# Two RMS norms from one set of squares, value projections in wider items, and narrow products in four column groups, in a two-block hybrid kernel

## The chip, the cores and the metric

One core of one Trainium2 chip runs the whole program. The metric is the device time of one execution in microseconds, the median over the runs. Smaller is better.

## What is computed

The reference is a first block of two layers (a gated delta rule mixer, GDN, and a state space mixer, SSD, each followed by an expert-choice mixture of 16 experts), a final RMS norm, and a second block, which begins with an RMS norm of its own. 512 tokens and 256 context tokens of width 1024 go through it in float32. What the change touches:

```python
def rms_norm(x, g):
    xf = x.astype(F32)
    y = xf * lax.rsqrt(jnp.mean(xf * xf, axis=-1, keepdims=True) + EPS)
    return (y * g.astype(F32)).astype(x.dtype)
...
# first block, GDN mixer: the last 32 columns of the input projection
beta = jax.nn.sigmoid(p[..., off:off + 2 * GDN_HEADS].astype(F32)).reshape(b, t, 2, GDN_HEADS)
off += 2 * GDN_HEADS
g = neg_a * jax.nn.softplus(p[..., off:].astype(F32).reshape(b, t, 2, GDN_HEADS) + dt_bias.astype(F32))
...
# first block, SSD mixer
y = y.reshape(b, t, SSD_INNER).astype(h.dtype) * jax.nn.silu(z)
return rms_norm(y, norm_g) @ w_out, hf, hb
...
# end of the first block, start of the second
x = rms_norm(x, final_norm_g)
h = rms_norm_2(x, mix_norm_g[i])
(u, c_b, c_c, c_x, q, k_c, v_c, k_s, v_s, k_w, v_w, nsa_gates, mix_gates) = split_projection(h @ w_in[i])
```

## The kernel before

The tokens lie in SBUF turned: width on the 128 partitions in eight tiles (`RT[:, k, :]`, k from 0 to 7), tokens along the free axis, 256 of the context and then 512. Each engine has one program written out by hand, and semaphores tie them together. SyncE loads the weights in the order of `weight_plan` (L111) into a ring of six slots; `slots` (L162) gives each item its slot and the item whose use frees it. TensorE takes the items in the same order (`take`). A float32 product appears in the trace as two records (two passes) for one matmul.

**Norms.** `norm_sums` (PE, L1153 to 1165) sums the squares over the partitions with a matmul by ones. The tokens are cut into quarters, and each quarter goes to one group of 32 array columns and 32 PSUM partitions, so that the four products of a k stand in four column groups. ScalarE squares the even k (`norm`, L2234) and VectorE the odd (`squares`), through a ring of four buffers. Then ScalarE takes the root (L2244), VectorE the reciprocal (`reciprocal_root`, L2822), `norm_spread` (PE, L1167 to 1175) spreads it over all partitions with products of 32 rows, and VectorE scales the eight tiles (L2833, or L3484 in the second block). Call 4 is the final norm, written over `RT`; call 5 the second block's mix norm, from `RT` into `h2`; call 6 is the norm ahead of the feed-forward part. GpSimd makes ten masks (L1065 to L1079) when call 5 has scaled; TensorE waits for `nstt` and then for `mask_done` before `values`.

**Values.** `values` (PE, L1948 to 1956) makes two value projections of 128 columns and the gates' 24, for four tiles of 128 tokens: item by item, each with 32 products (8 k for each of 4 token tiles) with the normed tokens as the loaded operand. ScalarE copies each of the three out when it is done (L2633, the last with a sigmoid, L2635). `queries_keys` waits for all three.

**GDN tail.** `gdn_tail` (PE, L1190 to 1197) projects the normed tokens onto 32 columns: for each k one product of 512 moving columns and one of 256, which fill 32 of the 128 array columns. It waits for ScalarE's `h_ready` of each k (L2262). ScalarE copies the result out (L2283, L2284), TensorE turns it after the first projection tile (L1203), VectorE takes it in (L2851, L2852). The projection tiles (L1238) follow.

**SSD output.** `ssd_out` on TensorE (L1898) makes 16 gate tiles (z, in split float32, lines L1744 to L1753) and after tile i the sum of squares of tile i-2: one product by a full matrix of ones, 512 columns (L1904). ScalarE applies SiLU (L2606), squares (L2612) and scales by the norm's gain (L2613); VectorE multiplies and splits. When all 16 are summed, ScalarE takes the root over 128x512 (L2615) and VectorE the reciprocal (L3456), while TensorE is already in the output products (`sout`, 48 matmuls for each of 8 tiles of the output width, L1894). VectorE applies the reciprocal to each tile's result (L3463) and adds it to `RT` (L3466).

The experts (`experts(1)`, L1595 and others) lie between the SSD output and the final norm.

## Time and profile before

| | us |
|---|---|
| median of 3 runs | 4127.23 |
| lowest and highest run | 4116.75, 4130.4 |
| profiled execution, span from first to last instruction | 4131.5 |
| TensorE busy | 3788.0 (92%) |
| VectorE busy | 1836.7 (44%) |
| ScalarE busy | 942.2 (23%) |
| GpSimd busy | 354.9 (9%) |
| TensorE weight load busy | 2328.2 (56%) |
| mean granted TensorE clock, of full | 0.956 |

The profile gives the span of its execution and not that execution's own total time, which includes what lies around the span. Busy shares are means over stages of different kinds, and a busy TensorE need not be at its peak: pipelined matmuls overlap. In the timeline a row is one instruction or a merged run of like ones: start, duration, engine, line, operation, operands, count and, in brackets, the idle time before it with what ended it.

### The profile page before, as it was taken

How to read it: one execution, taken by the hardware profiler on the slowest of the kernel's cores; microseconds unless marked ns; L12 is line 12 of the kernel's file. 1: busy time of each engine (PE TensorE's matmuls, PEld its weight loads, DVE VectorE, ACT ScalarE, POOL GpSimd, SP SyncE). 2: the span in 40 equal slices, each digit the busy share in tenths (PEclk: the TensorE clock that was granted, in tenths of full speed). 3: DMA queues.
4: the chain of work that ended last, by engine and by line, in shares of the span. 5: the costliest groups of instructions: out<-in, count | busy, mean ns of one | idle time of the engine just before them, and what ended most of it. 6: DMA issues, size and time to landing. Idle time of an engine off the chain costs nothing.

```text
span 4131.5 us, 50603 instructions
## 1 busy us (share of the span) xinstructions
PE 3788.0 (92%) x21228; PEld 2328.2 (56%) x21228; DVE 1836.7 (44%) x2915; ACT 942.2 (23%) x1862; POOL 354.9 (9%) x929
## 2 busy tenths in 40 slices
PE   7989999998999998999988988888698998998999
PEld 4578656865534443777766762222255433446777
DVE  3656456654012221588885530111326467415443
ACT  3421133123111011456564121000115100100000
POOL 0033002301000000000000000000040157000000
PEclk8989999998999999799999989999898999999999
DMA  5241131312598896212111429999721112231331
GB/s 199 84 127 47 51 132 56 119 63 83 224 384 337 337 369 245 100 57 82 52 41 41 133 93 381 421 421 421 270 78 41 34 50 57 75 102 51 102 102 51
DMA packets 278564, 631.29 MB, mean 153 GB/s; under 512 B 63553, under 2 KB 205377, under 8 KB 219457
## 3 DMA queue, kind: packets, MB, share of 16 engines
q1 hardware_dynamic: 275712, 627.40, 41.2%
q8 instruction: 168, 2.75, 0.3%
q10 hardware_dynamic: 2624, 0.66, 0.1%
q14 instruction: 60, 0.48, 0.0%
HBM read 611.75 MB, written 16.25 MB: 152 GB/s over the span
## 4 chain that ended last, share of the span: by engine, by line
PE 67%; DMA 11%; DVE 10%; ACT 3%; POOL 3%; SPq 3%; issue 3%; ACTq 0%; DVEq 0%
PE ps L1894 11%; PE ps L1595 11%; PE ps L1238 6%; PE ps L1945 5%; PE ps L1601 4%; DMA arena<-moe_w_down 4%; DMA arena<-moe_w_gate 2%; PE ps L1502 2%; PE ps L2118 2%; PE ps L1480 2%; PE ps L1753 2%; PE ps L1748 2%; PE ps L1744 2%; DMA arena<-moe_w_up 2%; DVE arena L3488 2%
## 5 line engine op out<-in xcount | busy, mean ns | idle before, releaser
L1595 PE MATMUL ps<-arena 128*64 128x512 f32 x3072 | 709.4, 601 | 79.3 <-DMA arena<-moe_w_down 23.0
L1595 PEld LDWEIGHTS ps<-arena 128*64 128x64 f32 x3072 | 207.4, 137 | 529.4 <-issue 385.2
L3225 DVE SCALAR_TENSOR_TENSOR arena<-arena,ps 128x512 f32<-128x512 f32 (+1 forms) x48 | 30.2, 656 | 525.1 <-PE ps L1595 525.1
L1238 PE MATMUL ps<-arena 128*128 128x512 f32 (+1 forms) x768 | 253.9, 489 | 3.5 <-DVE g_rows L2882 2.1
L1945 PE MATMUL ps<-arena 128*128 128x512 f32 x512 | 229.6, 605 | 5.0 <-DVE arena L3488 4.3
L3488 DVE TENSOR_TENSOR arena<-arena,ps 128x512 f32<-128x512 f32 x86 | 58.4, 687 | 372.4 <-ACT arena L2769 143.6
L1748 PE MATMUL ps<-h_first,w_rest 128*128 128x512 f32 (+1 forms) x576 | 208.9, 379 | 0.6 <-DVE arena L3384 0.5
L1238 PEld LDWEIGHTS ps<-arena 128*128 128x128 f32 x768 | 145.9, 191 | 105.8 <-issue 93.6
L3233 DVE TENSOR_TENSOR m_yx_rest<-ps,m_yx_lead 64x512 fp32r<-64x512 f32 x64 | 44.1, 689 | 363.0 <-ACT m_yc_lead L2484 205.6
L1744 PE MATMUL ps<-h_second,w_rest 128*128 128x512 f32 (+1 forms) x576 | 196.1, 355 | 0.4 <-DVE h_second L3291 0.4
L2484 ACT ACTIVATE m_yx_lead<-ps 64x512 fp32r<-64x512 f32 x64 | 37.8, 591 | 662.3 <-PE ps L1595 661.5
L1601 PE MATMUL ps<-arena 128*32 128x256 f32 x3072 | 175.7, 380 | 0.0
L1945 PEld LDWEIGHTS ps<-arena 128*128 128x128 f32 x512 | 98.9, 195 | 134.4 <-issue 127.1
L1894 PE MATMUL ps<-h_lead,w_lead 128*128 128x512 f32 x352 | 139.7, 397 | 11.4 <-DVE h_rest L3426 6.8
L1601 PEld LDWEIGHTS ps<-arena 128*32 128x32 f32 x3072 | 94.7, 109 | 96.8 <-issue 38.9
L1894 PE MATMUL ps<-h_rest,w_lead 128*128 128x512 f32 x352 | 139.5, 396 | 0.0
L1894 PE MATMUL ps<-h_lead,w_rest 128*128 128x512 f32 x352 | 139.1, 395 | 0.0
L1045 POOL IOTA arena<- 128x64 f32 x2 | 0.4, 185 | 1523.0 <-DVE arena L3466 1388.3
L3488 DVE TENSOR_TENSOR arena<-arena 128x512 f32<-128x512 f32 (+4 forms) x181 | 126.4, 738 | 6.2 <-ACT arena L2720 2.6
L1753 PE MATMUL ps<-h_first,w_rest 128*128 128x512 f32 (+1 forms) x576 | 124.6, 359 | 0.1
L1748 PEld LDWEIGHTS ps<-h_first,w_rest 128*128 128x128 f32 x576 | 110.0, 191 | 19.8 <-issue 3.5
L1744 PEld LDWEIGHTS ps<-h_second,w_rest 128*128 128x128 f32 x576 | 108.7, 189 | 18.9 <-issue 3.1
(496 smaller groups left out, 6990.6 us busy)
## 6 DMA issues: line engine op xcount, KB each, us to landing
arena<-moe_w_gate SPq DMA_DIRECT2D x128, 1024.0 KB, 9.3
arena<-moe_w_up SPq DMA_DIRECT2D x128, 1024.0 KB, 10.7
arena<-moe_w_down SPq DMA_DIRECT2D x128, 1024.0 KB, 11.8
arena<-ada_w SPq DMA_DIRECT2D x48, 1024.0 KB, 5.0
arena<-ffn_w_gate_up SPq DMA_DIRECT2D x22, 1024.0 KB, 5.0
arena<-gdn_w_in SPq DMA_DIRECT2D x16, 1024.0 KB, 8.9
arena<-w_in SPq DMA_DIRECT2D x30, 512.0 KB, 3.8
arena<-ssd_w_x SPq DMA_DIRECT2D x8, 1024.0 KB, 4.8
```

The costliest lines, as they stand in the source:

```text
L1238: mm = pe.matmul(ps[:, 2 * (i % 2) + j, 0:nn], state.w[:, k, m * P:(m + 1) * P], hT[:, k, c0:c0 + nn], start=(k == 0), stop=(k == KD - 1))
L1480: mm = pe.matmul(ps[:, 2 + b + 2 * (j % 2), 0:nn], state.w[:, k, (j % 2) * P:(j % 2) * P + P], hT[:, k, c0:c0 + nn], start=(k == 0), stop= ...
L1502: mm = pe.matmul(ps[:, b + 2 * (m % 2), 0:nn], w[j // 2][:, j % 2, m * P:(m + 1) * P], oT[:, j, c0:c0 + nn], start=(j == 0), stop=(j == HG ...
L1595: mm = pe.matmul(ps[CAPX * h:CAPX * h + CAPX, bank, :], x[:, 0:CAPX], w[:, 512 * h:512 * h + 512], **flags)
L1601: mm = pe.matmul(ps[CAPC * q:CAPC * q + CAPC, bank, 0:CW], x[:, CAPX:SLOTS], w[:, CW * q:CW * q + CW], **flags)
L1744: rests = lambda k: pe.matmul(out, wh[:, k, cols_], hT_lo[k][:, x], start=False, stop=(tail_last and k == KD - 1))
L1748: pe.matmul(out, wh[:, k, cols_], hT_hi[k][:, x], start=(k == 0), stop=False)
L1753: mm = pe.matmul(out, wl[:, k, cols_], hT_hi[k][:, x], start=False, stop=(not tail_last and k == KD - 1))
L1894: mm = pe.matmul(out, a[:, k, cols_], tile_of(b, k), start=(k == 0 and n == 0), stop=(k == tiles - 1 and n == 2))
L1945: mm = pe.matmul(ps[:, bank, :], w[:, k, i * P:(i + 1) * P], h2[:, k, :], start=(k == 0), stop=(k == KD - 1))
L2118: mm = pe.matmul(ps[:, (3 * i + x) % 5, :], w[:, k, (i % 2) * P:(i % 2 + 1) * P], h2[:, k, :], start=(k == 0), stop=(k == KD - 1))
L3488: v.do(dve.tensor_tensor(out, a_, b_, op), sem)
```

## The change

1. The final norm and the mix norm share one set of squares. TensorE sums the squares x² as before and beside it the squares weighed with the final gain squared (`weighed`, from `gain2`). From the first root VectorE and ScalarE work out the second one: the mean square of the final-normed tokens is the weighed sum times the first factor squared. Both factors are spread together; VectorE first scales into `h2` with the product of both gains, then `RT`. Calls are renumbered (6 becomes 5).
2. The second block's values come from two items of 4 k and 280 columns (128, 128 and 24 together), so that a product moves 280 columns, and all three results are copied out after the last of 32 products.
3. The SSD output norm sums the four quarters of the tokens in four column groups; root and reciprocal work on 128 columns, and after the first output product TensorE spreads the reciprocal by four products of 32 rows; ScalarE copies it from PSUM.
4. The GDN tail's products go token tile by token tile to four column groups.

```diff
-    plan += [("bv", n) for n in range(3)]
+    plan += [("bv", n) for n in range(2)]
...
+        tail_at = lambda t: (slice(32 * (t % 4), 32 * (t % 4) + 32), slice(t // 4 * P, t // 4 * P + P))
...
-            pool.wait_ge(s.nstt, nstt0[5] + KD)
+            pool.wait_ge(s.nstt, nstt0[4] + KD)
...
             def norm_sums(call, sets, weighed=None):
...
+                    for g in range(4 if weighed is not None else 0):
+                        r = slice(32 * g, 32 * g + 32)
+                        mm = pe.matmul(ps[r, 0, P:2 * P], weighed[:, k, :], nsqb[k % 4][:, CTX + g * P:CTX + g * P + P],
+                                       start=False, stop=(k == KD - 1))
...
             def norm_spread(call, sets):
-                for c0, w, at in quarters_of(sets):
+                for w, at in [(w, at) for _, w, at in quarters_of(sets)] + ([(P, P)] if call == 4 else []):
...
             def gdn_tail():
-                    for bank, (c0, nn, _) in ((2, XSET), (3, CSET)):
-                        mm = pe.matmul(ps[0:4 * GH, bank, 0:nn], w[:, k, :], hT[:, k, c0:c0 + nn], start=(k == 0), stop=(k == KD - 1))
+                    for t in range(NT):
+                        r, c = tail_at(t)
+                        mm = pe.matmul(ps[r, 2 + t // 4, 0:P], w[:, k, :], hT[:, k, t * P:(t + 1) * P], start=(k == 0), stop=(k == KD - 1))
...
             def ssd_out():
                 def sums(i):
-                    mm = pe.matmul(ps[:, 7, :], ones, z_sq[i % 2], start=(i == 0), stop=(i == 15))
+                    for g in range(4):
+                        r = slice(32 * g, 32 * g + 32)
+                        mm = pe.matmul(ps[r, 7, 0:P], ones[:, r], z_sq[i % 2][:, g * P:(g + 1) * P], start=(i == 0), stop=(i == 15))
+                def spread():
+                    pe.wait_ge(s.root_part, 1)
+                    for g in range(4):
+                        r = slice(32 * g, 32 * g + 32)
+                        mm = pe.matmul(ps[:, 4 + g, 0:P], ones[r, :], z_rs[r, :], start=True, stop=True)
+                    mm.then_inc(s.root_part, 1)
...
                     product(ps[:, m % 2, :], w, slice(0, P), (y_hi, y_lo), SI // P, split_ready).then_inc(s.w_used, 1)
+                    if m == 0:
+                        spread()
...
             def values():
-                for n in range(3):
-                    w = take(("bv", n))
-                    nn = (P, P, 3 * NH)[n]
-                    for t in range(4):
-                        for k in range(KD):
-                            mm = pe.matmul(ps[:, n, t * nn:(t + 1) * nn], h2[:, k, t * P:(t + 1) * P], w[:, k, :],
-                                           start=(k == 0), stop=(k == KD - 1))
-                    mm.then_inc(s.w_used, 1)
+                w = [take(("bv", n)) for n in range(2)]
+                for t in range(4):
+                    for k in range(KD):
+                        mm = pe.matmul(ps[:, t, 0:VALUES], h2[:, k, t * P:(t + 1) * P], w[k // 4][:, k % 4, :],
+                                       start=(k == 0), stop=(k == KD - 1))
+                mm.then_inc(s.w_used, 2)
             def queries_keys():
                 pe.wait_ge(s.bv_out, 3)
+                pe.wait_ge(s.nstt, nstt0[4] + 2 * KD)
...
-            norm_sums(4, (XSET,))
+            norm_sums(4, (XSET,), gain2)
             norm_spread(4, (XSET,))
-            norm_sums(5, (XSET,))
-            norm_spread(5, (XSET,))
...
# ScalarE
-            a.do(act.activation(tail[:, CTX:N], ps[0:4 * GH, 2, :], ACT.Copy))
-            a.do(act.activation(tail[:, 0:CTX], ps[0:4 * GH, 3, 0:CTX], ACT.Copy), s.tl_in)
+            a.do(act.activation(tail[:, 0:P], ps[:, 2, 0:P], ACT.Copy))
+            a.do(act.activation(tail[0:64, P:2 * P], ps[0:64, 3, 0:P], ACT.Copy), s.tl_in)
...
-                a.do(act.activation(z_rt, ps[:, 7, :], ACT.Sqrt, bias=epsc, scale=1.0 / SI), s.go_rt)
+                a.do(act.activation(z_rt, ps[:, 7, 0:P], ACT.Sqrt, bias=eps32, scale=1024.0 / SI), s.go_rt)
+                act.wait_ge(s.root_part, 2)
+                a.do(act.activation(z_all.rearrange("p (g c) -> p g c", g=4), ps[:, 4:8, 0:P], ACT.Copy), s.root_part)
...
+                act.wait_ge(s.w_used, USED[("bv", 1)])
+                for n in range(2):
+                    a.do(act.activation(vS[:, n, :, :], ps[:, 0:4, n * P:(n + 1) * P], ACT.Copy), s.bv_out)
+                a.do(act.activation(ng, ps[:, 0:4, 2 * P:VALUES], ACT.Sigmoid), s.bv_out)
...
             norm(4, (XSET,))
+            act.wait_ge(s.root_part, 4)
+            a.do(act.activation(nrtb[:, 2 * P:3 * P], nrtb[:, P:2 * P], ACT.Sqrt, bias=eps32, scale=1024.0 * 1024.0 / D), s.root_part)
             act.wait_ge(s.nstt, nstt0[4] + KD)
-            norm(5, (XSET,))
...
# VectorE, SSD output
-                v.do(dve.reciprocal(z_rs, z_rt))
-                v.settle()
+                v.do(dve.reciprocal(z_rs, z_rt), s.root_part)
...
-                    v.do(dve.tensor_tensor(z_tmp[m % 2], ps[:, m % 2, :], z_rs, ALU.mult))
+                    if m == 0:
+                        dve.wait_ge(s.root_part, 3)
+                    v.do(dve.tensor_tensor(z_tmp[m % 2], ps[:, m % 2, :], z_all, ALU.mult))
...
# VectorE, after route(1), before experts(1)
+            v.do(dve.tensor_tensor(gain2, col("final", 0, KD).unsqueeze(2).to_broadcast([P, KD, 32]), col("final", 0, KD).unsqueeze(2).to_broadcast([P, KD, 32]), ALU.mult))
+            v.do(dve.tensor_tensor(col("mixn", 0, KD), col("mixn", 0, KD), col("final", 0, KD), ALU.mult))
...
+            def two_norms():
+                squares(4, (XSET,))
+                dve.wait_ge(s.nrt, 3 * 4 + 1)
+                first, t, root2 = nrsb[:, P:2 * P], nrtb[:, P:2 * P], nrtb[:, 2 * P:3 * P]
+                v.do(dve.reciprocal(first, nrtb[:, 0:P]))
+                v.settle()
+                tt(t, ps[:, 0, P:2 * P], first, ALU.mult)
+                v.settle()
+                tt(t, t, first, ALU.mult, s.root_part)
+                dve.wait_ge(s.root_part, 5)
+                v.do(dve.reciprocal(nrsb[:, 2 * P:3 * P], root2))
+                v.settle()
+                v.do(dve.scalar_tensor_tensor(out=nrsb[:, 0:P], in0=nrsb[:, 2 * P:3 * P], scalar=32.0, in1=first, op0=ALU.mult, op1=ALU.mult), s.nrt)
+                dve.wait_ge(s.nrt, 3 * 4 + 3)
+                scaled_norm("mixn", 0, lambda k: h2[:, k, :])
+                v.settle()
+                scaled_norm("final", P, lambda k: RT[:, k, CTX:N])
```

VectorE's intake of the turned tail becomes four instructions (for the first four token tiles and the last two) in place of two.

## Rows read from the trace of the kernel before

**Rows 1.** The page's chain that ended last, by engine.

```profile
PE 67%; DMA 11%; DVE 10%; ACT 3%; POOL 3%; SPq 3%; issue 3%; ACTq 0%; DVEq 0%
```

**Rows 2.** Timeline, 24 to 92 us: start us, us, engine, line, what.

```profile
41.55 13.25 PE L1196 MATMUL ps<-arena 128*32 128x512 f32 x32
...
41.86 4.15 ACT L2262 ACTIVATE arena<-arena 128x512 f32<-128x512 f32 x8 [1.92 <-DVE arena L2797]
...
54.73 10.59 PE L1238 MATMUL ps<-arena 128*128 128x512 f32 x32
```

**Rows 3.** Windows: us, busy time of each engine, PEclk (granted clock), DMA share, GB/s.

```profile
46.00:48.00 2.00, 2.00 (x7) 0.59 (x5) 0.00 (x0) 0.01 (x1) 0.00 (x0) 0.72 0.98 371
```

**Rows 4.** Timeline of TensorE, SSD gate loop.

```profile
2213.10 2.02 PE L1753 MATMUL ps<-h_first,w_rest 128*128 128x512 f32 x8
...
2218.60 2.02 PE L1753 MATMUL ps<-h_first,w_rest 128*128 128x512 f32 x8
...
2224.96 2.02 PE L1753 MATMUL ps<-h_first,w_rest 128*128 128x512 f32 x8
```

**Rows 5.** Timeline, first product of the SSD output.

```profile
2309.32 0.50 PE L1894 MATMUL ps<-y_lead,so_lead 128*128 128x512 f32 x1 [2.48 <-DVE w_rest L3426]
```

**Rows 6.** Timeline, the two norms and the start of the values.

```profile
2969.25 2.48 PE L1164 MATMUL ps<-arena 128*32 128x128 f32 x64 [1.60 <-ACT arena L2241]
...
2972.20 0.37 ACT L2244 ACTIVATE arena<-ps,arena 128x128 f32<-128x128 f32 x1
2972.60 0.95 DVE L2822 RECIPROCAL arena<-arena 128x128 f32<-128x128 f32 x1 [1.35 <-ACT arena L2244]
...
2973.60 0.50 PE L1174 MATMUL ps<-arena 32*128 32x128 f32 x8 [1.88 <-DVE arena L2822]
...
2980.25 3.64 PE L1164 MATMUL ps<-arena 128*32 128x128 f32 x64 [6.14 <-ACT arena L2241]
...
2985.37 0.81 PE L1174 MATMUL ps<-arena 32*128 32x128 f32 x8 [1.48 <-DVE arena L2822]
2986.25 5.36 DVE L3484 SCALAR_TENSOR_TENSOR arena<-arena,ps 128x512 f32<-128x512 f32 x8 [0.94 <-PE ps L1174]
...
2993.74 25.60 PE L1954 MATMUL ps<-arena 128*128 128x128 f32 x192 [7.56 <-issue]
```

**Rows 7.** Timeline, the end of the values and the first query product.

```profile
3011.12 0.60 ACT L2633 ACTIVATE arena<-ps 128x512 f32<-128x512 f32 x1 [6.55 <-PE ps L1954]
...
3011.74 1.28 ACT L2635 ACT_TABLE_LOAD   x1
...
3019.37 0.25 ACT L2635 ACTIVATE arena<-ps 128x96 f32<-128x96 f32 x1 [6.35 <-PE ps L1954]
...
3019.68 1.22 PE L1973 MATMUL ps<-arena 128*128 128x512 f32 x1 [0.34 <-ACT arena L2635]
```

**Rows 8.** Timeline of TensorE, a block in four column groups between other products.

```profile
103.62 1.46 PE L1238 MATMUL ps<-arena 128*128 128x256 f32 x6
105.01 1.93 PE L1141 MATMUL ps<-arena 128*32 128x256 f32 x32
106.88 1.12 PE L1247 MATMUL ps<-arena 128*128 128x512 f32 x2
```

**Rows 9.** Lines by form: an operation of 128 columns of VectorE on PSUM.

```profile
L3011 DVE SCALAR_TENSOR_TENSOR arena<-ps,arena 128x128 f32<-128x128 f32 x96 | 27.1, 344 | 6.9 <-PE ps L1382 6.9
```

**Rows 10.** Timeline of VectorE, first operation after the experts' start.

```profile
2501.38 0.75 DVE L3225 SCALAR_TENSOR_TENSOR arena<-arena,ps 128x512 f32<-128x512 f32 x1 [38.38 <-PE ps L1595]
```

**Rows 11.** Windows, start and end of the values: columns as rows 3.

```profile
2995.00:3000.00 5.00, 5.00 (x27) 5.00 (x27) 3.92 (x28) 1.52 (x3) 0.94 (x7) 0.54 0.00 0
3018.00:3020.00 2.00, 1.66 (x8) 1.54 (x8) 0.00 (x0) 0.25 (x1) 1.92 (x2) 0.50 0.00 0
```

**Rows 12.** Windows, then waits of SyncE's queue, in the second experts' stage.

```profile
2600.00:2700.00 100.00, 85.56 (x366) 28.32 (x366) 14.73 (x21) 7.13 (x12) 0.00 (x0) 1.00 1.01 421
...
SPq L888 <- ACT arena L2458: 56.0, 1, 56.0
```

More of the change, by code:

```diff
@@ L52 @@
 NST = 16
+VALUES = 2 * 128 + 3 * NH
 TURN = 6.2831850
@@ L315, in __init__ @@
         self.s_st = new("s_st")
+        self.root_part = new("root_part")
         self.sz_act = new("sz_act")
@@ L709, in source2 @@
             if kind == "bv":
-                a, w = ((WVS, P), (WVW, P), (WNG, 24))[item[1]]
-                return whole(win[:, :, a:a + w])
+                k = slice(4 * item[1], 4 * item[1] + 4)
+                return [((lambda w: w[:, :, 0:P]), win[:, k, WVS:WVS + P]), ((lambda w: w[:, :, P:VALUES]), win[:, k, WVW:WVW + P + 3 * NH])]
             if kind == "bq":
@@ L751, in shape_of @@
                 return (4, HD)
+            if item[0] == "bv":
+                return (4, VALUES)
             if item[0] == "glu":
@@ L1151, in ada_turn, with norm_sums @@
                 mm.then_inc(s.ada_cols, 1)
-            def norm_sums(call, sets):
+            def norm_sums(call, sets, weighed=None):
                 parts = quarters_of(sets)
@@ L1164, in norm_sums @@
                             mm = pe.matmul(ps[r, 0, at:at + w], ones[:, r], nsqb[k % 4][:, c0 + g * w:c0 + g * w + w],
-                                           start=(k == 0 and at == 0), stop=(k == KD - 1 and at == parts[-1][2]))
+                                           start=(k == 0 and at == 0), stop=(k == KD - 1 and at == parts[-1][2] and weighed is None))
+                    for g in range(4 if weighed is not None else 0):
+                        r = slice(32 * g, 32 * g + 32)
+                        mm = pe.matmul(ps[r, 0, P:2 * P], weighed[:, k, :], nsqb[k % 4][:, CTX + g * P:CTX + g * P + P],
+                                       start=False, stop=(k == KD - 1))
                     mm.then_inc(s.nsq_sum, 1)
@@ L1202, in gdn_tail_turned @@
                 for t in range(NT):
-                    mm = pe.transpose(ps[:, 6, 32 * t:32 * t + 32], tail[:, t * P:(t + 1) * P], ident[0:4 * GH, 0:4 * GH])
+                    r, c = tail_at(t)
+                    mm = pe.transpose(ps[:, 4 + t % 4, 32 * (t // 4):32 * (t // 4) + 32], tail[r, c], ident[r, r])
                 mm.then_inc(s.tl_in, 1)
@@ L2784, in _ @@
             act.wait_ge(s.resid, RES_SSD + KD)
-            norm(6, (XSET,))
+            norm(5, (XSET,))
             ffn()
@@ L2850, in _ @@
             dve.wait_ge(s.tl_in, 2)
[L2851 to L2853 removed]
+            for t0, nt in ((0, 4), (4, 2)):
+                turned = ps[:, 4:4 + nt, 8 * t0:8 * t0 + 32]
+                v.do(dve.tensor_copy(betag[:, t0:t0 + nt, 0:16], turned[:, :, 0:16]))
+                v.do(dve.tensor_tensor(betag[:, t0:t0 + nt, 16:32], turned[:, :, 16:32],
+                                       col("gdtb", 0, 16).unsqueeze(1).to_broadcast([P, nt, 16]), ALU.add), s.tl_bias if t0 else None)
             dve.wait_ge(s.tl_act, 1)
@@ L3475, in _, with scaled_norm @@
             route(1)
+            v.do(dve.tensor_tensor(gain2, col("final", 0, KD).unsqueeze(2).to_broadcast([P, KD, 32]), col("final", 0, KD).unsqueeze(2).to_broadcast([P, KD, 32]), ALU.mult))
+            v.do(dve.tensor_tensor(col("mixn", 0, KD), col("mixn", 0, KD), col("final", 0, KD), ALU.mult))
+            v.settle()
             experts(1)
-            def norm2(call, gain, dst):
-                if call != 6:
-                    squares(call, (XSET,))
-                reciprocal_root(call, (XSET,))
+            def scaled_norm(gain, at, dst):
                 for k in range(KD):
-                    v.do(dve.scalar_tensor_tensor(out=fours(dst(k)), in0=fours(RT[:, k, CTX:N]), scalar=col(gain, k), in1=spread_root(SEQ // 4, 0),
+                    v.do(dve.scalar_tensor_tensor(out=fours(dst(k)), in0=fours(RT[:, k, CTX:N]), scalar=col(gain, k), in1=spread_root(SEQ // 4, at),
                                                   op0=ALU.mult, op1=ALU.mult), s.nstt)
+            def two_norms():
[13 more added lines that the diff above has]
+                scaled_norm("mixn", 0, lambda k: h2[:, k, :])
+                v.settle()
+                scaled_norm("final", P, lambda k: RT[:, k, CTX:N])
             def tt(out, a_, b_, op, sem=None):
@@ L3792, in ffn @@
                         split(f[:, i % 8, :], tile_of(f_hi, i), tile_of(f_lo, i), s.ff_hid)
-            norm2(4, "final", lambda k: RT[:, k, CTX:N])
-            norm2(5, "mixn", lambda k: h2[:, k, :])
+            two_norms()
             dve.wait_ge(s.mask_done, MASKS + 10)
@@ L3803, in _ @@
             mix()
-            squares(6, (XSET,))
+            squares(5, (XSET,))
             split_unit(0)
-            norm2(6, "ffnn", lambda k: h2[:, k, :])
+            reciprocal_root(5, (XSET,))
+            scaled_norm("ffnn", 0, lambda k: h2[:, k, :])
             ffn()
```

23 lines of the change are left out of this document (7 added, 16 removed).

## The prediction

> **What bounds the kernel now.** I read the page's chain by engine first [rows 1]: TensorE carries 67% of it, DMA 11%, VectorE 10%. So a change on TensorE counts in full unless a stage between is set by DMA. The change touches four places, and I read each in the timeline, in order of time. The granted clock I took from the windows, because TensorE's durations double when it falls: 1.00 is 2.4 GHz, 0.50 is 1.2 GHz.
>
> The GDN tail [rows 2] is a block of 32 records from 41.55 us, and the first projection tile follows it at 54.73. That tile moves just as many columns (16 records of 512 and 16 of 256, 12288 in all) and lasts 10.59 us, or 0.86 ns for a column of a record. I use this rate at full clock throughout. The tail took 13.2 us because the clock was low until about 47.1 (a mean of 0.72 over 46 to 48, [rows 3]).
>
> In the SSD gate loop a tile without a sum takes 5.50 us (2213.10 to 2218.60) and one with a sum 6.36 (to 2224.96) [rows 4]: a sum costs 0.86. There TensorE never stops. After the loop it waits 2.48 us for VectorE's splitting of the first output weight [rows 5].
>
> Between the blocks everything is a relay. The first norm's sums start at 2969.25, the second norm's last scaling ends at 2991.61, and the wait for GpSimd's masks, which the code puts behind it, holds TensorE until 2993.74 [rows 6]. Then 192 records of values take until 3019.36 and the queries start at 3019.68 [rows 6, 7].
>
> **GDN tail.** The same products go to four groups of 32 array columns, six tiles of 128 tokens per k. That four groups run side by side is in the trace: 32 records of 256 columns take from 105.01 to 106.88 [rows 8], 1.87 us, where 8192 columns in line would take 7.0. Six tiles need two rounds, so a k costs 2 x 2 x 128 x 0.86 = 0.44 us at full clock, 0.88 at the low one. Starting at 41.55 with the clock low to 47.1, 6.3 of the 8 k's are done by then and the other 1.7 take 0.75: end 47.9, and I give the projection 48.0. ScalarE's h tiles end at 46.01 [rows 2], so they allow this. Gain 54.73 - 48.0 = 6.7. Bounds: 7.7 if only h limits it (46.01 plus one k), and 4.3 if the clock stays low another 3.4 us, which costs 0.7 in the tail and 1.7 in the tile behind. The tail's copies on ScalarE shrink and two instructions more on VectorE (under 0.3 us each) sit in its long wait; its next step is held by TensorE's second tile, so all that shifts as one. The later weights need the tail's slot earlier, and get it.
>
> **SSD norm.** A sum becomes four products of 128 columns, 8 records: 8 x 128 / 4 x 0.86 = 0.22 us. Row evidence on going into the narrow shape and out: six records of 256 columns from 103.62 should end at 104.94 and the grouped block begins at 105.01, 0.07 late; the block itself holds 1.75 us of work and takes 1.87, 0.12 more [rows 8]. So 0.42 per sum, 0.44 less. Sums 0 to 12 stand ahead of the last gate product, so 13 x 0.44 = 5.7. The last three hide behind VectorE's split, which keeps its 2.48 us wait. New on the path is the spreading behind the first output product: 8 records, 0.50 [rows 6], and 0.2 for changing shape, 0.7. The reciprocal shrinks to a quarter of its columns and ScalarE's copy of 512 columns (0.60, [rows 7]) comes in; VectorE waits for it, but TensorE needs its result only before the third output product, and the whole second one lies between, so both cost nothing. If that cover went, they would cost 0.6. Net 5.0. Bounds: 7.8 with no price for changing shape, and a loss of 0.7 if each sum costs what it did.
>
> The page "TensorEngine Tiling (Array Packing)" of the Trainium skill, section Tiling Modes, says that changing the tiling mode drains TensorE. The rows just read show 0.2 us for both changes together, which is compatible with a drain and small; were a full drain to eat the saving of every sum, the sum over all parts would be that of the first rival below.
>
> **Final norm and mix norm.** Removed: a second round of squares, sums, root and spreading, and the second block of eight scalings (5.36) from the path, since the final scaling now runs behind the mix one, beside the values. Added on the path, by steps from 2969.25: 128 records of sums instead of 64, at full clock 8 x 0.44 = 3.5 and 0.25 to finish, 2973.0 (the old ones, 2.48 us, were paced by the squares; the root stood ready at 2972.20 behind its table load, so 0.8 later). Root 0.37, reciprocal 0.95, two multiplies of 128 columns at 0.34 (nearest row, a VectorE operation of that size on PSUM [rows 9]), second root 0.37, second reciprocal 0.95, one more 0.34, and 0.05 at each of seven handovers: 4.0, so 2977.0. Spreading two sets at the clock that by then is low: 0.81 for one [rows 6], 1.25 for two. Eight scalings 5.36: 2983.7. Gain 2991.6 - 2983.7 = 7.9. Bounds: 8.7 with the spreading at full clock and cheap multiplies, 3.3 if the sums run at the low clock (3.64 for 64 records [rows 6], 7.3 for 128) and the multiplies cost double. GpSimd's masks still start after the mix norm, so their 2.1 us stay, now beside VectorE's final scaling: 0 to 2 us more; I take 0. The two gain products before the experts fall in a gap of VectorE of 38 us [rows 10]; cost 0. VectorE's preparation for the S5 part starts behind the final scaling, about as early as before, and its user, the S5 part, comes only behind the attention.
>
> **Values.** 64 records of 280 columns: 64 x 280 x 0.86 = 15.4 us. The clock was low from before 2993.74 to about 2999.7 (0.54 in [rows 11]); a wait of the same kind precedes it, so I keep 6 us at half speed, 3.0: 18.4. But all three copies come after the last product, where two were hidden: 2 x 0.60, the table load 1.28, the sigmoid 0.25 and handovers, 2.8 us in which TensorE stands, for 0.3 before [rows 7]. The old block of 24 columns ended at low clock (0.50 [rows 11]) and the queries began so; the new stall probably leaves them a similar start, so they cost the same. 25.94 - 18.4 - 2.8 = 4.7. Bounds 7.7 (full clock from the start) and 1.7 (low clock for 6 us more).
>
> The page "ScalarE: Activation LUTs" of the Trainium skill, section What ACT_TABLE_LOAD costs, adds about 1.38 us of drain to a load of 1.28. The row of the load and its neighbours show 1.28 with the next operation free at once; with the page's drain this part would give 3.3 and not 4.7.
>
> **Sum.** 6.7 + 5.0 + 7.9 + 4.7 = 24.3 us. The profiled execution has a span of 4131.5; its own total is not shown, and the span is 4.3 over the median of the runs, 4127.2. From the span I get 4107.2, from the median 4102.9. I forecast 4103.
>
> **The rivals.**
> 1. *Changing shape eats the sums.* SSD then gives -0.7 and not 5.0: 4108.5. For it: 26 changes in a loop with no slack. Against: the 0.2 us read from [rows 8]. Chance 0.12.
> 2. *The clock stays low longer* behind the tail, in the norm and behind the values' stall: by the lower bounds of three parts 4.3 + 5.0 + 3.3 + 1.7 = 14.3: 4113. Chance 0.12.
> 3. *The experts' DMA absorbs what comes before it.* In that stage the queues run at 421 GB/s, share 1.01, and TensorE waits for them [rows 12]. If the stream's start were fixed, the 11.7 us of tail and SSD would vanish: 4114.5, no measurable change or just faster. Against: SyncE waits 56 us for ScalarE's last copy of the routing before the stream can run [rows 12], and that copy moves with TensorE. Chance 0.06.
> 4. *Slower: the gate loop falls to the low clock.* Its place is the sixteen gate tiles, 94 us of TensorE at 5.9 each, at the pace of the full clock now. If the shape changes in each tile brought the clock down, each microsecond at 1.2 GHz would cost half of one; from 49 us of low clock on the change loses, and with the whole loop low it takes 94 us more: 4197. Against: the grouped block of [rows 8] ran at the pace of the full clock, and so did what followed it. Chance 0.04.
> 5. *The groups do not overlap where PSUM banks are shared by six tiles:* tail 0, SSD -3.9, norm near 0, values 4.7: 4126. The block of [rows 8] is nearly proof against it; 0.02.
>
> **How the numbers follow.** The forecast has 0.64 (4095 to 4108). A measurement here tells about 0.3%, 12.4 us, from no change: faster means under 4114.8. Forecast and rivals 1 and 2, with most of 3, are on that side, the upper ends of 2 and 3 and rival 5 within it. The range takes in all upper bounds (7.7 + 7.8 + 8.7 + 7.7 = 31.9: 4095) with 5 us under them for the spread of the runs (4116.75 to 4130.4), so 4090; up to 4117 it holds rivals 1, 2 and 3, and leaves out little more than both low cases at once (4.3 - 0.7 + 3.3 + 1.7 = 8.6: 4119) and rivals 4 and 5.
>
> **What would show it.** Tail 6 to 7 us long with the first tile at about 48; gate tiles every 5.9 us; from the first sum to the last mix scaling 14.5 us (22.4 before), with two roots and one spreading in it; values 18 us, then a gap of 2.8 with the table load in it. Gate tiles still at 6.3 speak for rival 1, a clock of 0.50 in their windows for 4, a saving at the first expert product that is gone at the last for 3. The forecast is wrong if the spans of these four stages do not shrink by 20 us together.

## The result, and the profile after

The changed kernel takes 4108.85 us (median of 11 runs, 4096.63 to 4120.73), the kernel before 4130.95 on the same chip (11 runs, 4116.75 to 4139.22). The ratio is 0.9945, 95% interval [0.9932, 0.9958]: 22.1 us less, where 24.3 had been worked out. One execution further below, of the changed kernel run again, was in a slower state of the chip (4170.65 us, granted clock 0.912) and counts in no number. The profiled execution took 4111.48 us and has a span of 4109.5, 22.0 less than the span before. Its mean granted clock is the same, 0.956.

The page after (busy times of the engines, and the chain by engine). TensorE is busy 21.0 us less (3788.0 before) in a span that is 22.0 shorter; its share of the chain is what it was [rows 1]:

```profile
span 4109.5 us, 50683 instructions
PE 3767.0 (92%) x21268; PEld 2313.8 (56%) x21268; DVE 1833.0 (45%) x2918; ACT 940.0 (23%) x1859; POOL 354.8 (9%) x929
...
PE 67%; DMA 11%; DVE 10%; POOL 3%; ACT 3%; SPq 3%; issue 3%; ACTq 0%; DVEq 0%
```

**GDN tail.** Timeline after, to set against [rows 2] (start, duration, engine, line, operands, count):

```profile
43.09 6.26 PE L1207 MATMUL ps<-arena 128*32 128x128 f32 x96
...
49.28 10.59 PE L1250 MATMUL ps<-arena 128*128 128x512 f32 x32
```

From the first tail product to the first projection tile it is 6.19 us, before 13.18 (41.55 to 54.73). The stage gave 7.0. It started 1.5 us later than before, although nothing ahead of it had changed. That comes with the execution: the kernel with the norms alone, whose tail is the old one, starts it at 43.17, and the changed kernel with its sums in pairs at 41.96. In windows of the same trace the clock is 0.50 over 40 to 47 us and 0.65 over 47 to 49: nearly the whole tail still ran at 1.2 GHz, and four groups side by side made it short all the same.

**SSD gate loop and its sums.** Timeline of TensorE after, to set against [rows 4] and [rows 5]:

```profile
2217.20 2.02 PE L1765 MATMUL ps<-h_first,w_rest 128*128 128x512 f32 x8
...
2283.95 2.02 PE L1765 MATMUL ps<-h_first,w_rest 128*128 128x512 f32 x8
2285.91 0.43 PE L1918 MATMUL ps<-arena 128*32 128x128 f32 x8
2286.26 0.50 PE L1760 MATMUL ps<-h_first,w_rest 128*128 128x512 f32 x1
2286.60 0.39 PE L1756 MATMUL ps<-h_second,w_rest 128*128 128x512 f32 x1
...
2296.09 2.02 PE L1765 MATMUL ps<-h_first,w_rest 128*128 128x512 f32 x8
...
2304.05 0.79 PE L1906 MATMUL ps<-y_lead,so_lead 128*128 128x512 f32 x1 [3.18 <-DVE w_rest L3449]
```

L1765 at 2217.20 is the end of the last tile without a sum, 2296.09 that of the sixteenth: 78.89 us for 13 tiles, 6.07 each. A tile without a sum takes 5.50 here too, so a sum costs 0.57 (0.86 before). It can be seen where: the eight products of a tile's last group take 1.86 us, so they are done with at 2285.81; the group starts 0.10 later, the next gate product starts at 2286.26, 0.45 later, and the one behind it 0.34 after that instead of 0.23. From the same mark of the loop to the first output product it is 90.72 us before (2218.60 to 2309.32) and 86.85 now: 3.9 less. The first output product still waits for VectorE's split, now 3.18 us instead of 2.48. It comes 7.96 us after the mark of the sixteenth tile in both kernels (2301.36 to 2309.32 before, 2296.09 to 2304.05): what stands behind the last gate tile is covered by that wait.

**The norms.** Timeline after, to set against [rows 6]; the sums of the two norms alternate (L1170 the plain ones, L1174 the weighed ones, 0.43 us for a block of eight):

```profile
2963.79 0.43 PE L1170 MATMUL ps<-arena 128*32 128x128 f32 x8 [1.60 <-ACT arena L2262]
2964.01 0.43 PE L1174 MATMUL ps<-arena 128*32 128x128 f32 x8
...
2967.55 0.37 ACT L2265 ACTIVATE arena<-ps,arena 128x128 f32<-128x128 f32 x1 [0.25 <-PE ps L1174]
2967.95 0.95 DVE L3517 RECIPROCAL arena<-arena 128x128 f32<-128x128 f32 x1 [1.45 <-ACT arena L2265]
...
2969.59 0.40 ACT L2795 ACTIVATE arena<-arena 128x128 f32<-128x128 f32 x1 [1.67 <-DVE arena L3532]
...
2971.01 0.29 DVE L3525 SCALAR_TENSOR_TENSOR arena<-arena 128x128 f32<-128x128 f32 x1
2971.36 1.24 PE L1184 MATMUL ps<-arena 32*128 32x128 f32 x16 [3.86 <-DVE arena L3525]
2972.66 10.75 DVE L3508 SCALAR_TENSOR_TENSOR arena<-arena,ps 128x512 f32<-128x512 f32 x16 [1.36 <-PE ps L1184]
...
2978.08 0.16 POOL L1071 MEMSET arena<- 128x64 f32 x1 [553.26 <-DVE arena L3508]
...
2980.16 5.14 PE L1976 MATMUL ps<-arena 128*128 128x280 f32 x13 [7.56 <-DVE arena L3508]
```

Half of the sixteen scalings end at 2972.66 + 10.75/2 = 2978.03, and GpSimd starts its masks 0.05 later. From the first sum to there it is 14.2 us, before 22.4 (2969.25 to 2991.61). The wait for the masks is still behind it, 2.1 us.

**Values.** The values and the query products in the timeline of TensorE (192 records in 25.60 us before, then 0.3 us of idling, [rows 6, 7]):

```profile
2980.16 17.17 PE L1976 MATMUL ps<-arena 128*128 128x280 f32 x64 [7.56 <-DVE arena L3508]
3000.06 29.43 PE L1996 MATMUL ps<-arena 128*128 128x512 f32 x64 [2.74 <-ACT arena L2656]
```

ScalarE's rows between them:

```profile
2997.36 1.08 ACT L2655 ACTIVATE arena<-ps 128x512 f32<-128x512 f32 x2 [9.52 <-PE ps L1976]
2998.46 1.28 ACT L2656 ACT_TABLE_LOAD   x1
2999.76 0.25 ACT L2656 ACTIVATE arena<-ps 128x96 f32<-128x96 f32 x1
```

The windows of every engine behind them (columns: length, busy time and count of TensorE, its weight loads, VectorE, ScalarE, GpSimd; granted clock; DMA share; GB/s):

```profile
3000.00:3002.00 2.00, 1.94 (x4) 0.88 (x5) 0.00 (x0) 0.01 (x1) 1.76 (x5) 0.73 1.15 320
3002.00:3004.00 2.00, 2.00 (x4) 0.96 (x3) 0.00 (x0) 0.00 (x0) 1.84 (x4) 0.50 0.17 40
```

64 records take 17.2 us, then TensorE stands 2.7 us, and the queries start at 3000.06, 19.9 us after the values (25.94 before). The clock is 1.00 up to 3000 and falls inside the next window: some of the first query products ran at 1.2 GHz, as the first ones did before, where the clock had fallen already in the products of 24 columns (0.68 over 3016 to 3018, ahead of the idling). The 64 query records take 29.4 us, and 29.6 before.

**The sum.** Tail 7.0, norms 8.1, values 6.0, and SSD 3.2 (3.9 in the loop less the spreading, below) make 24.3 us; the span is 22.0 shorter. The rest is in stages that the change does not touch. From the first projection tile to the first router product it is 928.0 us before and 931.3 after. This is no matter of the clock, which is low for about 3 us less there; TensorE is idle 4.6 us longer, and its waits that end with the transfer into `low_in` (a small matrix of the GDN layer that goes out to memory and back) come to 8.3 us and not 3.2. The changed kernel is ahead by 5.5 us at the first projection tile, 2.1 at the router, 1.4 at the mark of the gate loop, 5.3 at the first output product, 5.5 at the end of the experts, 13.6 at the values, 19.6 at the queries and 22.0 at the end.

### The profile page after: what moved, and what is told of

It is laid out like the page before. It is cut to its first block, busy times and chain, and to the rows that moved or that the text cites. A ratio compares the mean times of both kernels' runs of the same rounds, so it can differ in the third digit from the quotient of the medians.

```text
span 4109.5 us, 50683 instructions
## 1 busy us (share of the span) xinstructions
PE 3767.0 (92%) x21268; PEld 2313.8 (56%) x21268; DVE 1833.0 (45%) x2918; ACT 940.0 (23%) x1859; POOL 354.8 (9%) x929
## 4 chain that ended last, share of the span: by engine, by line
PE 67%; DMA 11%; DVE 10%; POOL 3%; ACT 3%; SPq 3%; issue 3%; ACTq 0%; DVEq 0%
PE ps L1607 11%; PE ps L1906 11%; PE ps L1250 6%; PE ps L1969 5%; PE ps L1613 4%; DMA arena<-moe_w_down 4%; DMA arena<-moe_w_gate 2%; PE ps L1514 2%; PE ps L2141 2%; PE ps L1492 2%; PE ps L1765 2%; PE ps L1760 2%; PE ps L1756 2%; DMA arena<-moe_w_up 2%; DVE arena L3532 2%
## 5 line engine op out<-in xcount | busy, mean ns | idle before, releaser
L3532 DVE TENSOR_TENSOR arena<-arena 128x512 f32<-128x512 f32 (+3 forms) x182 | 126.0, 732 | 3.7 <-ACT arena L2746 0.7
L1765 PE MATMUL ps<-h_first,w_rest 128*128 128x512 f32 (+1 forms) x576 | 124.7, 359 | 0.2
```

What stands on the lines that cost most here:

```text
L1765: mm = pe.matmul(out, wl[:, k, cols_], hT_hi[k][:, x], start=False, stop=(not tail_last and k == KD - 1))
L3532: v.do(dve.tensor_tensor(out, a_, b_, op), sem)
```

## The experiments

Four kernels are the kernel before with one part of the change each, timed together (kernel before: median 4132.41 of 35 runs). Of each, the stage is read in the trace and the whole from the runs.

### The GDN tail alone

```diff
-                    for bank, (c0, nn, _) in ((2, XSET), (3, CSET)):
-                        mm = pe.matmul(ps[0:4 * GH, bank, 0:nn], w[:, k, :], hT[:, k, c0:c0 + nn], ...)
+                    for t in range(NT):
+                        r, c = tail_at(t)
+                        mm = pe.matmul(ps[r, 2 + t // 4, 0:P], w[:, k, :], hT[:, k, t * P:(t + 1) * P], ...)
```

> Only the GDN tail of the change (column groups, its copies and turning), all else as before. Theory (each part's gain at its place is kept to the end): from the tail's first product to the first projection tile 6 to 7 us instead of 13.2, and a ratio of 0.9983, 7 us less, about at the edge of what can be told. Rival (the gain is given back between the second head group and the experts, where the lead over the kernel before fell from 6.5 us at 660 to 2.1 us at 980): the same 6 to 7 us at the tail, but a lead of 2 us at the router product near 980 and a ratio of 0.9995.

4122.8 us (12 runs), ratio 0.9979 [0.9967, 0.9991]. Timeline:

```profile
42.63 6.23 PE L1198 MATMUL ps<-arena 128*32 128x128 f32 x96
48.80 10.59 PE L1241 MATMUL ps<-arena 128*128 128x512 f32 x32
```

6.2 us again, 7.0 less. From the first projection tile to the router's first product this kernel needs 927.7 us, as little as before (928.0). The whole change needs 931.3; so does the kernel with the norms alone (931.7), whose tail is the old one; SSD alone needs 927.6, values alone 927.5. In the further kernels below, all with the new tail, it is 924.5 to 931.2 us. The 3.3 us that the whole change seemed to give back there come and go with the execution and do not belong to the tail. The reason is not the same each time: against the kernel before, the norms alone had some 12 us more of low clock there and the same waits for `low_in` (3.4 us); the changed kernel had the longer waits. The rival, a lead of 2 us at the router product, fell: here it is 6.2 us (976.5 against 982.7).

### The SSD output norm alone

```diff
-                    mm = pe.matmul(ps[:, 7, :], ones, z_sq[i % 2], start=(i == 0), stop=(i == 15))
+                    for g in range(4):
+                        r = slice(32 * g, 32 * g + 32)
+                        mm = pe.matmul(ps[r, 7, 0:P], ones[:, r], z_sq[i % 2][:, g * P:(g + 1) * P], ...)
```

> Only the SSD output norm of the change. Theory: a gate tile every 6.05 to 6.09 us instead of 6.36, a lead of 3.9 us gained from the second gate tile to the first output product, of which the spreading behind it takes 0.7 to 1.2; 3 us in all, ratio 0.9992. Rival (the shape changes bring the clock down or cost all that the sums save): tiles of 6.3 us, no lead, ratio 1.000 or over.

4127.48 us, ratio 0.9991 [0.9979, 1.0002]. From the first record of the first sum to the start of the last record of the last it is 81.4 us, as in the whole change; 85.7 before and 85.8 in the three kernels without this part. From the mark ahead of the first sum to the first output product it is 86.85 us again (2219.65 to 2306.50), 3.9 less. The runs alone cannot tell this from none, the stage can.

### The norms alone

```diff
-            norm_sums(4, (XSET,))
+            norm_sums(4, (XSET,), gain2)
...
-            norm_sums(5, (XSET,))
-            norm_spread(5, (XSET,))
-            pe.wait_ge(s.nstt, nstt0[5] + KD)
+            pe.wait_ge(s.nstt, nstt0[4] + KD)
```

> Only the two norms from one set of squares, values as before. Theory: from the squares' first operation to the end of the mix norm's scalings 15.0 us instead of 23.1, values as long as before (25.6 to 26), ratio 0.9980. Rival (the shorter relay leaves the values another clock or lets VectorE's final scaling disturb them): the values take 2 us more or less than 25.6, and the ratio is 0.9985 or 0.9975.

4122.75 us, ratio 0.9978 [0.9966, 0.9989]. Timeline (squares, spreading, weight load of the values):

```profile
2969.92 1.15 ACT L2246 ACTIVATE arena<-arena 128x512 f32<-128x512 f32 x2 [13.36 <-DVE arena L3261]
...
2978.26 1.24 PE L1180 MATMUL ps<-arena 32*128 32x128 f32 x16 [3.86 <-DVE arena L3506]
...
2987.03 3.27 PEld L1960 LDWEIGHTS ps<-arena 128*128 128x128 f32 x15 [7.83 <-DVE arena L3489]
```

From the squares' start to the values it is 17.1 us, as in the whole change (2963.02 to 2980.16); before, 25.3 (2968.48 to 2993.74). The stage gives 8.1 by itself. The values behind it take 25.6 us as before, so the rival fell.

### The values alone

```diff
-                for n in range(3):
-                    w = take(("bv", n))
...
+                w = [take(("bv", n)) for n in range(2)]
+                for t in range(4):
+                    for k in range(KD):
+                        mm = pe.matmul(ps[:, t, 0:VALUES], h2[:, k, t * P:(t + 1) * P], w[k // 4][:, k % 4, :], ...)
```

> Only the values in two items of 280 columns, norms as before. Theory: products 17 to 18 us, then a gap of 2.7 us before the queries, 19.9 us instead of 25.9, ratio 0.9985. Rival (the gain of the values needs the clock that the shorter norms leave): products over 20 us, ratio 0.9993.

4126.96 us, ratio 0.9985 [0.9973, 0.9997]. Timeline:

```profile
2987.47 17.10 PE L1955 MATMUL ps<-arena 128*128 128x280 f32 x64 [7.57 <-issue]
...
3007.31 2.16 PE L1974 MATMUL ps<-arena 128*128 128x512 f32 x3 [2.74 <-ACT arena L2634]
```

19.8 us to the queries (25.94 before): 6.1 less. The product of the four ratios is 0.9933, the ratio of the whole 0.9945 [0.9932, 0.9958]: the parts add up within what the runs can tell, and in the stages they add up to a tenth.

The four kernels that follow change one thing in the changed kernel. They have one time each (4103 to 4109 us), which proves nothing; what is read is their stages, each in one execution.

### What a sum costs without the change of shape

```diff
-                    for g in range(4):
-                        r = slice(32 * g, 32 * g + 32)
-                        mm = pe.matmul(ps[r, 7, 0:P], ones[:, r], z_sq[i % 2][:, g * P:(g + 1) * P], ...)
+                    mm = pe.matmul(ps[:, 7, 0:P], ones, z_sq[i % 2][:, 0:P], start=(i == 0), stop=(i == 15))
```

> The changed kernel, but the SSD sums are one product of the whole array over the first quarter of the tokens; the other three quarters are left out, so the norm is not the reference's. The same 128 columns go through the array as in four groups side by side, without a change of the array's shape. Theory (of the 0.57 us that a sum costs now, 0.22 is columns and 0.35 the two changes of shape): a gate tile every 5.75 us, 13 tiles 4 us shorter than with groups. Rival (the price is in leaving fp32r products for fp32 ones, whatever the shape): a tile every 6.0 us.

Three quarters of the tokens are left out of the sum. Timeline of TensorE:

```profile
2218.53 2.03 PE L1765 MATMUL ps<-h_first,w_rest 128*128 128x512 f32 x8
2220.39 0.38 PE L1916 MATMUL ps<-arena 128*128 128x128 f32 x2
2220.53 0.48 PE L1760 MATMUL ps<-h_first,w_rest 128*128 128x512 f32 x1
2220.85 0.40 PE L1756 MATMUL ps<-h_second,w_rest 128*128 128x512 f32 x1
...
2224.40 2.03 PE L1765 MATMUL ps<-h_first,w_rest 128*128 128x512 f32 x8
```

A tile takes 5.87 us, between the two expectations. At the place of the sum itself it costs 0.23 (0.14 for its own rows, and the gate product behind it takes 0.32 instead of 0.23), what 2 x 128 columns cost by the rate of the prediction, 0.22. The other 0.14 is spread over the tile behind: its fifteen products start 0.237 apart (from 2220.85 to 2224.40), where they start 0.227 to 0.229 apart behind a sum in four groups and in the kernel before. Why a full-array sum slows the tile behind it is not shown. Taken at its own place, then, the sum without the change costs 0.23 and the one with it 0.56 (0.45 for its rows and 0.11 on the product behind, read in the changed kernel above): the change of shape, there and back, costs 0.33. Taken over whole tiles the difference is smaller, 0.57 against 0.37, as the tile behind the single group is not slowed: from the third tile to the sixteenth this kernel needs 76.3 us and the changed one 78.9, 2.6 less where the theory said 4.

### Sums in pairs

```diff
-                    if i >= 2:
+                    if i >= 3 and i % 2:
+                        sums(i - 3)
                         sums(i - 2)
```

> The changed kernel with the sums of squares taken in pairs, after every second gate tile, so that half of the changes of shape go. Theory (0.35 us for a change there and back): the loop from the first to the last sum is 2.3 us shorter, each pair costing 0.8. Rival (it is a price of each sum and not of the change): the same time as in the changed kernel, two tiles and two sums in 12.1 us.

Timeline of TensorE:

```profile
2220.13 2.02 PE L1765 MATMUL ps<-h_first,w_rest 128*128 128x512 f32 x8
...
2225.63 2.02 PE L1765 MATMUL ps<-h_first,w_rest 128*128 128x512 f32 x8
2227.58 0.64 PE L1918 MATMUL ps<-arena 128*32 128x128 f32 x16
2228.15 0.50 PE L1760 MATMUL ps<-h_first,w_rest 128*128 128x512 f32 x1
...
2232.04 2.03 PE L1765 MATMUL ps<-h_first,w_rest 128*128 128x512 f32 x8
...
2297.15 2.02 PE L1765 MATMUL ps<-h_first,w_rest 128*128 128x512 f32 x8
```

Two sums in one block cost 6.41 - 5.50 = 0.91 us, 0.46 each instead of 0.57. The loop, from the third tile to the sixteenth (2220.13 to 2297.15), takes 77.02 us instead of 78.89: 1.9 less, where 2.3 was expected and the rival said none. Not all of it is the price of the shape. The loop now holds six pairs, twelve sums, where thirteen stood; the thirteenth stands behind the sixteenth tile, where TensorE's wait for VectorE covers it (3.19 us, as in the changed kernel). Moving it gives 0.6, and the six pairs give 1.3, about 0.22 each. At its own place a pair costs 0.77, that is 2 x 0.22 for its columns and 0.33 for one change there and back; the tile behind is again slower by 0.14, which takes back 0.8 us over the six pairs. At its own place both runs give the same price for the change of shape, and since eight more records in a block add no more than their columns, it is not a price of the number of instructions.

### The copies of the values per token tile

```diff
-                act.wait_ge(s.w_used, USED[("bv", 1)])
-                for n in range(2):
-                    a.do(act.activation(vS[:, n, :, :], ps[:, 0:4, n * P:(n + 1) * P], ACT.Copy), s.bv_out)
-                a.do(act.activation(ng, ps[:, 0:4, 2 * P:VALUES], ACT.Sigmoid), s.bv_out)
+                for t in range(4):
...
+                    a.do(act.activation(vS[:, :, t, :], ps[:, t, 0:2 * P].rearrange(...), ACT.Copy), s.bv_out)
+                    a.do(act.activation(ng[:, t, :], ps[:, t, 2 * P:VALUES], ACT.Sigmoid), s.bv_out)
```

> The changed kernel with the values copied out token tile by token tile, so that the table load of the sigmoid and three quarters of the copies stand beside products. Theory: the gap of 2.74 us before the queries shrinks to 0.7, and the granted clock does not fall to 0.50 behind it, so that the queries are 1 to 1.5 us shorter too: 3.5 us in all. Rival (the clock falls for the idle time before the values and not for this gap): the queries as long as before, 2.0 us in all.

Timeline (the table load comes with the first token tile, beside the products):

```profile
2988.12 1.28 ACT L2661 ACT_TABLE_LOAD   x1
...
2997.57 0.38 ACT L2660 ACTIVATE arena<-ps 128x256 f32<-128x256 f32 x1 [3.31 <-PE ps L1976]
...
2998.08 6.28 PE L1998 MATMUL ps<-arena 128*128 128x512 f32 x14 [0.55 <-ACT arena L2661]
```

The gap is 0.55 us instead of 2.7, the queries start 17.9 us after the values (19.9), and the clock behind it stays at 1.00, so that the query products take 27.7 us and not 29.4. The first 2.0 are the copies'. The other 1.7 are not theirs by necessity: the kernel that follows had the full gap of 2.74 us and no fall behind it either (27.7), while the changed kernel, the one with the values alone and the two kernels above had the gap and the fall (29.4 in each).

### GpSimd's masks ahead of the norms

```diff
-            pool.wait_ge(s.nstt, nstt0[4] + KD)
+            pool.wait_ge(s.sc_free, 64)
...
-            a.do(act.activation(nrtb[:, 2 * P:3 * P], ...
+            a.do(act.activation(nrsb[:, 3 * P:4 * P], ...
```

> The changed kernel with GpSimd's masks made as soon as the experts are done, and the second root kept in another piece of SBUF, so that the two do not meet. Theory (the 2.1 us behind the mix norm are this wait alone): the values begin within 0.1 us of the last mix scaling, 2.0 us earlier. Rival (GpSimd and VectorE share a way to SBUF): the norms on VectorE get longer by more than 1 us while the masks are made, and the gain is under 1 us.

Timeline:

```profile
2959.59 1.15 ACT L2262 ACTIVATE arena<-arena 128x512 f32<-128x512 f32 x2 [13.34 <-DVE arena L3279]
...
2959.61 0.16 POOL L1071 MEMSET arena<- 128x64 f32 x1 [535.43 <-DVE arena L3279]
...
2969.23 10.75 DVE L3508 SCALAR_TENSOR_TENSOR arena<-arena,ps 128x512 f32<-128x512 f32 x16 [1.36 <-PE ps L1184]
...
2974.64 6.67 PE L1976 MATMUL ps<-arena 128*128 128x280 f32 x15 [5.48 <-DVE arena L3508]
```

The values start 0.03 us after the last mix scaling (2969.23 + 5.38) and 15.0 us after the squares' start instead of 17.1: 2.1 less. None of VectorE's steps became longer, so the rival fell; GpSimd's own four selections (L1076), now beside VectorE's squares, took 1.19 us in place of 0.66. But half of it is given back in the next stage. The first products then fall on more of the low clock (0.50 in the windows up to 2980, 0.95 over 2980 to 2985: 5.9 us of it, for 3.7 us in the changed kernel, by 0.53 over 2982 to 2984), and the values take 18.2 us and not 17.2 (18.3 in the combination below).

### The three together, against the changed kernel

> The changed kernel with the three edits of the single runs together: the sums of the SSD output norm in pairs, the copies of the values per token tile, GpSimd's masks ahead of the norms with their own place for the second root. Measured one by one these gave 1.9 us in the gate loop, 1.7 us at the gap (3.1 to 1.0 us, as far as the clock stays as it is) and 2.0 us before the values. Nothing that one of them frees is used by another, so if single savings add up, as the four parts of the change did, the kernel takes 5.6 us less than the changed one on the same chip, and up to 7.3 where the clock no longer falls behind the gap: a ratio to the kernel before of 0.9928 to 0.9932, where the changed kernel gives 0.9945. The rival: a stage behind (the queries' weights or the attention's preparation on GpSimd and VectorE) takes up what the values give, and the gain is under 2 us: ratio 0.994 or more.

> The changed kernel again, unaltered, to stand beside the combination on the same chip: ratio 0.9945, 22 to 23 us less than the kernel before, 4 stages of 6.2, 81.4, 14.3 and 19.9 us for the tail, the loop of sums, the norms and the values with their gap, all within 0.2 us unless the clock's stretches lie otherwise.

All on one chip (kernel before: 4128.93). The combination takes 4099.56 us (6 runs, 4094.34 to 4105.6), ratio 0.9928 [0.9913, 0.9944]; the changed kernel 4109.5 (median of 6 runs, 4101.0 to 4113.08), ratio 0.9955 [0.9939, 0.9971]. Timeline of the combination:

```profile
2959.37 1.15 ACT L2265 ACTIVATE arena<-arena 128x512 f32<-128x512 f32 x2 [13.39 <-DVE arena L3285]
...
2993.23 3.27 PE L1999 MATMUL ps<-arena 128*128 128x512 f32 x7 [0.56 <-ACT arena L2662]
```

From the squares to the queries it is 33.9 us (37.0 in the changed kernel), the queries take 27.7 instead of 29.4, and the gate loop is 1.9 shorter: 6.7 us by the stages, inside the 5.6 to 7.3 expected. The medians are 9.9 apart; of the 3.2 beyond the stages nothing in the trace tells whether they are more than the spread of six runs. It beats both kernels, and the rival (less than 2 us) is out. The stages of the repeated changed kernel are not read again; that they hold is seen in the single parts above.

## Why the prediction was right

The forecast, 4103 with a range of 4090 to 4117, stands 5.9 us below the 4108.85 measured. Of these, 3.7 lie in the start: it counts from the median of three runs of the kernel before (4127.23), and that of all eleven is 4130.95. The other 2.2 are the gain, 24.3 against 22.1. By its own steps:

- **What bounds the kernel.** Held. Each of the four savings, made alone, shortens its own stage by as much as in the whole change, and the span follows. No stage behind, the one bound by DMA included, took one up.
- **GDN tail, 6.7.** Measured 7.0. The projection was given 48.0 from a start at 41.55; it came at 49.28 from a start at 43.09. The clock rose about 5.3 us into the tail (0.65 over 47 to 49), where 5.5 had been assumed. The lower bound of 4.3 counts its 3.4 us of low clock twice: at half speed they cost 1.7 in all, 0.7 in the tail and 1.0 in the tile behind, so by its own terms it is 5.0, and rival 2 comes to 4112 and not 4113. No row gives the length of 3.4 us.
- **SSD norm, 5.0.** The term that was most mis-sized: 3.2. The step that failed is "So 0.42 per sum". What it read from [rows 8] came nearly as read: the group starts 0.10 late (0.07), and from its start to the next gate product it is 0.35 us (0.34). What it put at nothing is the first product behind the group: the one after it starts 0.34 later and not 0.23, 0.11 lost. So a sum costs 0.57, and 13 of them give 3.9 and not 5.7. The bound on the other side, no gain, was right to keep. The spreading was priced at 0.7: in the trace the four products come at 2317.17 and the next output tile 0.53 us later than it would, its first product 0.11 longer, 0.64 in all. TensorE's wait for VectorE's split grew from 2.48 to 3.18, as TensorE, which before had larger last sums to do, now idles in their place. The reciprocal and ScalarE's copy cost nothing, as given: no output product waits for them.
- **The rule on the tiling mode.** Against the full-array sum of the same 128 columns the group loses 0.10 us ahead of it (2285.81 to 2285.91, where that sum starts at once, 2220.39) and 0.21 from its start to the next gate product (0.35 against 0.14); the 0.11 on that product is hardly the change's, as it is 0.09 behind the full-array sum too. The idle 0.10 agrees with the Trainium skill, "TensorEngine Tiling (Array Packing)", section Tiling Modes, by which a change of mode drains TensorE; that the rest is a drain is not shown. The 0.33 us together take half of the 0.64 that the groups save in columns (0.86 less 0.22). Rival 1, by which they would take all, fell: a tile takes 6.07, not 6.3.
- **Norms, 7.9.** Measured 8.1. First sum to last mix scaling 14.2 against 14.5. The sums took 3.7 us to the root, as given. The steps from the first root to the spreading took 3.8 for 4.0, the scaling of the second factor among them 0.29 for 0.34 (L3525); the spreading took 1.24 for 1.25. The masks' wait stayed at 2.1 as said, beside VectorE's final scaling, and was not longer.
- **Values, 4.7.** Measured 6.0. The products took 17.2 us for 18.4, as the low clock lasted 3.7 us into them and not 6. The stall was 2.7 for 2.8: copies 1.08, load 1.28, sigmoid 0.25, handovers. The prediction took from [rows 7] that the operation behind the load was free at once; these rows do not show it, as the sigmoid waited for TensorE until 6.35 us after the load. The rows after do. The Trainium skill, "ScalarE: Activation LUTs", section What ACT_TABLE_LOAD costs, adds 1.38 us of drain to a load; here the load starts 0.02 after the copy's end (2998.44) and the sigmoid 0.02 after the load's (2999.74), so no drain stands in this gap.
- **The sum, 24.3.** By the stages it is 24.3 again, with SSD 1.8 lower and the other three 1.8 higher together. That is luck in the sizes and not in the places. The span gave 22.0, and the runs 22.1.
- **Rival 2, the clock low longer.** It did not come in any of its three places. The clock fell behind the values' stall, as it had before without one, and the query products took as long (29.4 and 29.6).
- **Rival 3, the experts' DMA.** Fell. At the first output product the changed kernel is 5.3 us ahead (2304.05 against 2309.32). The end of the experts, in the timeline of TensorE, is in the kernel before and in the changed one

```profile
2953.80 0.73 PE L1669 MATMUL ps<-rank,owner 16*128 16x512 f32 x2
```

```profile
2948.34 0.73 PE L1681 MATMUL ps<-rank,owner 16*128 16x512 f32 x2
```

still 5.5 us ahead, with the queues at 420 GB/s in both [rows 12]. SyncE waits 56.0 us for ScalarE's copy in both kernels before the stream runs, so the stream's start moved with TensorE's work, as the prediction had argued.
- **Rival 4, the gate loop at the low clock.** Fell. The gate tiles keep 5.50 us between sums and the windows show 1.00 from 2206 on, with and without narrow products.
- **Rival 5, no overlap where banks are shared.** Fell. The tail at 6.2 us and the alternating sums at 0.22 us for eight records show four groups side by side.

## What to carry to other kernels

Products that fill 32 of 128 columns are worth putting side by side, even singly between full-array ones, but here each excursion cost about a third of a microsecond at its own place, and a fifth counted over the whole tile: collect them in as few blocks as the data allows. Wider copies that wait for the last product expose what narrow ones hid, the table load above all; do them by tile. And time saved in a wait of TensorE can be partly paid back: of the 2.1 us that the early masks saved, 1.0 went to products that then fell on the low clock.

## What the runs showed that was not expected

- A stall of 2.7 us of TensorE ahead of the queries was followed by the low clock in the changed kernel and in those with the values alone, with one quarter and with pairs, and not in the one with the masks ahead. Stalls of 0.55 us were followed by 1.00 in both kernels that had them. What decides it is open.
- The stretch of low clock at the start of the values was 3.7 us in the changed kernel, 5.9 in the one with the masks ahead and about 6 before, with the same kind of wait ahead of it.
- A full-array float32 sum of 128 columns slows the fifteen gate products behind it from 0.228 to 0.237 us each (0.14 per tile), and so does a pair of sums in four groups; a single one in four groups, 0.43 us of rows, does not. Which property makes the difference was not tried.
- A stage that the change does not touch, from the first projection tile to the router, takes 924.5 to 931.7 us in eleven kernels. TensorE's waits for the transfers into `low_in` in it range from 1.7 to 8.3 us, the stretches at the low clock from about 51 to 72 us in all.
